# Turning the attention's value product round: probabilities stationary, values moving, the division after the product

## The chip, the cores and the metric

The kernel runs on one core of a Trainium2 chip. The metric is the device time of one execution in microseconds (us), as a median over several executions. One core has TensorE (PE; its weight loads are listed apart as PEld), VectorE (DVE), ScalarE (ACT), GpSimd (POOL) and SyncE (SP), which here issues the DMAs. Each engine takes its instructions in program order and waits on semaphores.

## What is computed

Two groups of rows, 1024 prompt rows and 32 sample rows, run through one attention layer and one gated linear recurrence, with norms and output projections around them. All is fp32. The part that matters is the core of the attention, for 8 query heads of width 128 that share 2 key and value heads (4 query heads each):

```python
logits = jnp.einsum('btkgd,btskd->btkgs', qg, k_sel).astype(f32) * ATT_SCALE
logits = jnp.where(valid[:, :, None, None, :], logits, -jnp.inf)
probs = jax.nn.softmax(logits, axis=-1).astype(v.dtype)
o = jnp.einsum('btkgs,btskd->btkgd', probs, v_sel)
...
return (o.reshape(B, L, ATT_WIDTH) * jax.nn.silu(z)) @ w_out
```

Each row attends to the 256 (sample: 136) keys that an indexer picks. The kernel does this densely with a mask, over all keys up to the row's block.

## The kernel before, in words

The program is a row of stages, each a block that ends before the next begins: input norm, attention projections (with the index scores and the search of the thresholds), attention, attention output, recurrence, final output. The change is in `attention`.

The stage walks over 72 items: 9 row tiles t (8 of 128 prompt rows, t = 0 to 7, and the sample's 32 rows, called tile S below), and 8 heads in each. A prompt tile t sees t+1 blocks of 128 keys, the sample 4 cached blocks and one of 32 keys. Every engine runs one loop over steps i, written out by hand, and works in step i on items that lie further and further back:

- PE, step i: the logits of item i (`multiply`, L843; q stationary, keys move, into `wide`); the transposes of the probabilities of item i-4 (`transpose`, L856, one per key block, into banks 0 and 1); and a quarter of a value product (`mix`, L872). `mix` works on a group of 4 heads that share a value head: v's block of 128x128 is stationary, and the four heads' transposed probabilities, 4x128 columns, move. The product comes out transposed (value column by row), as the output projection needs it.
- DVE, step i: `shift(i)` (L929) adds the mask, writes the row of logits to the SBUF ring `probs` and takes its extreme; then one of eight operations of `marking`, which makes the next tile's mask (L905 to L919); then `divide(i-2)`: a reciprocal of one column (L937) and a product of the whole row of probabilities with it (L939); every fourth step `gate` (L945), which multiplies a group's output in PSUM with the gate path.
- ACT, step i: the exponential of item i with its sum (L969), then the copies of the transposed probabilities of item i-4 from PSUM to `pT` (L979).

`multiply(i)` waits for `shift(i-2)`, since there are two halves of `wide`; `transpose` waits for `divide`; `mix` waits for the copies of its group. SP loads each tile's q and, once, the output weights. POOL works in this stage on two pieces of weights only (L200).

Of the kernel before, what the change touches and what calls it, by code (L numbers as in the profile page):

```python
# [16 lines left out]
ALU = mybir.AluOpType  # L17
# [757 lines left out]
def attention(nc, S):  # L775
# [23 lines left out]
    inv_done, probs_ready, pT_ready, pT_out = sem("inv_done"), sem("probs_ready"), sem("pT_ready"), sem("pT_out")  # L799
# [8 lines left out]
    q = space("q_tile", [P, 2, HEADS, P])  # L808
    with nc.Block() as block:
# [20 lines left out]
        def _(pe):  # L830
# [16 lines left out]
            def transpose(i):  # L847
                t, h = items[i]
                r = rows(t)
                pe.wait_ge(probs_ready, i + 1)  # L850
# [9 lines left out]
            def mix(g, quarter):  # L860

                t, h = items[4 * g]
                kv, r = h // GROUP, rows(t)
                if quarter == 0:
                    pe.wait_ge(pT_out, first_bank[4 * g + 4])
                    if g >= 2:
                        pe.wait_ge(gated, g - 1)
                n = (keys(t) + P - 1) // P
                for j in range((n * quarter + 3) // 4, (n * (quarter + 1) + 3) // 4):
                    kr = key_rows(t, j)  # L870
                    src = cv[:, j] if t == SAMPLE and j < PAST // P else v[0:kr, SAMPLE if t == SAMPLE else j]
                    last = pe.matmul(ps[2 + g % 2][:, 0:4 * r].rearrange("p (g q) -> p g q", g=4),  # L872
                                     src[:, kv * HD:(kv + 1) * HD], pT[0:kr, g % 2, j, :, 0:r],
                                     start=j == 0, stop=j == n - 1)
                    if j == n - 1:
                        last.then_inc(mixed, 1)

            for i in range(N + LAG + 4):
                if i < N:
                    multiply(i)  # L880
                if 0 <= i - LAG < N:
                    transpose(i - LAG)
                if i >= LAG + 4:
                    mix((i - LAG - 4) // 4, (i - LAG) % 4)

        @block.vector
        def _(dve):
# [45 lines left out]
            def divide(i):  # L933
                t, h = items[i]
                r, n = rows(t), keys(t)
# [13 lines left out]
            for i in range(N + 12):  # L949
# [7 lines left out]
                if 2 <= i <= N + 1:  # L957
                    divide(i - 2)
# [864 lines left out]
```

## Time and profile before

| | |
|---|---|
| three executions | 1550.73, 1551.94, 1554.93 us; median 1551.94 |
| profiled execution, first to last instruction (span) | 1547.9 us |
| granted TensorE clock, mean over the span | 0.960 of full speed |
| busy, share of the span | PE 91%, PEld 79%, DVE 62%, ACT 36%, POOL 33% |
| attention, first logits to last gate | 496.7 to 689.7 us, 193.0 us |
| PE busy in it | 181.2 us |
| DVE busy in it | 154.5 us |

Of the profiled execution the page gives its span; what lies outside the first and last instruction is the 4.0 us between it and the median, and nothing else of it is shown. A row of the profile gives an engine, a line of the program, an operation, the tiles it writes and reads, a count and durations. PE's durations are modelled ends of pipelined instructions, so the pace of a run of them is read from the starts.

### The profile page before, as it was taken

The numbers are of one execution on the slowest core, as the hardware profiler recorded it, in microseconds if no ns is written. First come the engines' busy times: TensorE is split into PE (matmuls) and PEld (weight loads), VectorE is DVE, ScalarE is ACT, GpSimd is POOL, SyncE is SP. The second block draws the span as 40 slices with busy tenths as digits, with TensorE's granted clock in tenths as the row PEclk, the third lists the DMA queues.
The fourth block names the chain that finished last, engine by engine and source line by source line (L and its number), as shares of the span: only waits on it lengthen the run. The fifth ranks groups of instructions, "written<-read, shape, count | busy, mean of one in ns | idle before, by whom it ended". The sixth has DMA issues, their size and how long they took to land. (4 is left out here: it accounts for less than half of the span.)

```text
span 1547.9 us, 21333 instructions
## 1 busy us (share of the span) xinstructions
PE 1402.9 (91%) x8109; PEld 1224.0 (79%) x8109; DVE 965.9 (62%) x1864; ACT 560.5 (36%) x1004; POOL 508.8 (33%) x404
## 2 busy tenths in 40 slices
PE   4999999999993899999979999999999999925898
PEld 3999647999992455548869999999999999914686
DVE  7011488999998989744550466475665566596332
ACT  6233463333322555541121444342525253340111
POOL 4276402355541001100020364544536163363000
PEclk9999999999996999999999999999999999957899
DMA  6121100232211410002231111010211110500221
GB/s 217 28 55 41 28 1 15 78 95 85 65 53 42 149 28 14 4 28 82 82 89 43 56 29 47 28 61 20 61 41 42 36 40 20 193 4 1 82 99 62
DMA packets 96180, 86.78 MB, mean 56 GB/s; under 512 B 4528, under 2 KB 84272, under 8 KB 96080
## 3 DMA queue, kind: packets, MB, share of 16 engines
q1 hardware_dynamic: 94448, 80.60, 16.9%
q0 software_dynamic: 1632, 4.82, 0.9%
q8 instruction: 66, 1.08, 0.3%
q14 instruction: 34, 0.28, 0.1%
HBM read 65.43 MB, written 19.97 MB: 55 GB/s over the span
## 5 line engine op out<-in xcount | busy, mean ns | idle before, releaser
L186 PE MATMUL bank<-hn_hi,rw_hi 128*128 128x352 f32 x768 | 250.3, 326 | 2.9 <-PEq L1009 2.9
L186 PE MATMUL bank<-hn_hi,rw_lo 128*128 128x352 f32 x768 | 247.2, 322 | 0.0
L186 PE MATMUL bank<-hn_lo,rw_hi 128*128 128x352 f32 x768 | 246.9, 322 | 0.0
L186 PE MATMUL bank<-hn_hi,w_hi 128*128 128x352 f32 x672 | 218.9, 326 | 3.6 <-PEq L274 3.6
L186 PE MATMUL bank<-hn_lo,w_hi 128*128 128x352 f32 x672 | 216.5, 322 | 0.0
L186 PE MATMUL bank<-hn_hi,w_lo 128*128 128x352 f32 x672 | 216.4, 322 | 0.0
L714 DVE TENSOR_SCALAR_CACHE_REDUCE marks<-score,bits 128x384 bf16<-128x384 f32 (+6 forms) x217 | 185.1, 917 | 3.7
L186 PEld LDWEIGHTS bank<-hn_hi,rw_hi 128*128 128x128 f32 x768 | 144.6, 188 | 4.6 <-POOL rw_lo L1145 3.1
L186 PEld LDWEIGHTS bank<-hn_lo,rw_hi 128*128 128x128 f32 x768 | 145.0, 189 | 0.0
L186 PEld LDWEIGHTS bank<-hn_hi,rw_lo 128*128 128x128 f32 x768 | 144.6, 188 | 0.0
L186 PEld LDWEIGHTS bank<-hn_hi,w_hi 128*128 128x128 f32 x672 | 127.0, 189 | 4.3 <-issue 3.7
L186 PEld LDWEIGHTS bank<-hn_lo,w_hi 128*128 128x128 f32 x672 | 127.2, 189 | 0.0
L186 PEld LDWEIGHTS bank<-hn_hi,w_lo 128*128 128x128 f32 x672 | 126.8, 189 | 0.0
L641 POOL TENSOR_TENSOR swapped<-swapped,sin 128x352 f32<-128x352 f32 x57 | 54.0, 947 | 187.8 <-ACT swapped L589 122.1
L1573 DVE TENSOR_TENSOR levels<-levels,q_rec 128x528 f32<-128x528 f32 (+1 forms) x48 | 101.4, 2177 | 1.9 <-ACT levels L1409 1.9
L843 PE MATMUL wide<-kT,q_tile 128*128 128x512 f32 (+3 forms) x192 | 75.4, 506 | 27.1 <-DMA q_tile<-q_rotated 26.9
L239 POOL TENSOR_SCALAR stats<-stats 128x1 f32<-128x1 f32 (+1 forms) x27 | 7.4, 273 | 279.4 <-ACT junk L1116 162.6
L1328 PE MATMUL wide<-levels 128*128 128x128 f32 (+1 forms) x832 | 98.2, 274 | 0.6
L1328 PEld LDWEIGHTS wide<-levels 128*128 128x128 f32 (+1 forms) x832 | 92.7, 185 | 6.0 <-issue 0.9
L1145 POOL TENSOR_TENSOR rw_lo<-rw_raw,rw_hi 128x1024 fp32r<-128x1024 f32 x32 | 76.0, 2386 | 59.6 <-ACT rw_hi L1138 59.5
L215 POOL TENSOR_TENSOR w_lo<-w_raw,w_hi 128x1024 fp32r<-128x1024 f32 x30 | 71.7, 2390 | 50.4 <-ACT w_hi L208 50.3
L843 PEld LDWEIGHTS wide<-kT,q_tile 128*128 128x128 f32 x192 | 36.6, 202 | 65.1 <-issue 34.2
(221 smaller groups left out, 2823.2 us busy)
## 6 DMA issues: line engine op xcount, KB each, us to landing
rw_raw<-in_rec_w_in SPq DMA_DIRECT2D x32, 512.0 KB, 4.1
w_raw<-in_att_w_in SPq DMA_DIRECT2D x30, 512.0 KB, 3.9
q_rotated<-relu SPq DMA_DIRECT2D x24, 176.0 KB, 1.9
xin<-in_x_prompt SPq DMA_DIRECT2D x8, 512.0 KB, 4.2
q_tile<-q_rotated SPq DMA_DIRECT2D x8, 512.0 KB, 3.7
wo_raw<-in_att_w_out SPq DMA_DIRECT2D x4, 1024.0 KB, 9.1
x_again<-in_x_prompt SPq DMA_DIRECT2D x8, 512.0 KB, 4.0
residual<-h_rows SPq DMA_DIRECT2D x8, 512.0 KB, 2.9
```

Source lines behind the costliest of these rows:

```text
L186: last = pe.matmul(out, l, r, start=n == 0, stop=n == len(passes) - 1)
L215: pool.tensor_tensor(S["w_lo"][:, slot], S["w_raw"][:, slot], S["w_hi"][:, slot].bitcast(F32), ALU.subtract).then_inc(S["w_lo_done"], 1)
L239: pool.tensor_scalar(stats[0:r, 1, t:t + 1], stats[0:r, 0, t:t + 1], 1.0 / D, EPS, ALU.mult, ALU.add).then_inc(pool_order, 1)
L641: pool.tensor_tensor(swapped[:, r % 3, :], swapped[:, r % 3, :], sin[:, part * CW:(part + 1) * CW], ALU.mult).then_inc(sin_done, 1)
L714: step(dve.tensor_scalar(marks[0:r, i % 2, 0:keys(t)], tile(i, t), bound, 0.0, op, ALU.add, accum_out=counts[0:r, first + i:first + i + 1]))
L843: last = pe.matmul(logits[0:rows(t), i % 2, a:e], q[:, t % 2, h, 0:rows(t)], src[:, h // GROUP, a:e], start=True, stop=True)
L1145: pool.tensor_tensor(S["rw_lo"][:, slot], S["rw_raw"][:, slot], S["rw_hi"][:, slot].bitcast(F32), ALU.subtract).then_inc(S["rec_lo_done"], 1)
L1328: last = pe.matmul(out[:, 0:r], left, right, start=True, stop=True)
L1573: dve.tensor_tensor(x, x, level_view(q[:, slot], m)[:, :, 1, :], ALU.mult).then_inc(q_scaled, 1)
```

## The change

The value product is done per head and not per group. For each head and key block the transposed probabilities (keys by 128 rows) are stationary and the 128 value columns move, so that the output stands row by value column in a quarter of the group's bank. The probabilities are no longer divided: `divide` now takes four reciprocals at once for a group, and a new DVE operation `scale` multiplies the group's output by them on its way from PSUM to `o_rows`. PE then turns the four 128x128 blocks back with four transposes (`turn`) into the same bank, from which `gate` reads as before. `transpose` waits for the exponential itself. The lags change too: `mix(i-6)` for one item in each step, `turn` in every fourth step, `divide`, `scale` and `gate` at other places of DVE's loop, and PE has one step more.

```diff
@@ PE @@
             def transpose(i):
-                pe.wait_ge(probs_ready, i + 1)
+                pe.wait_ge(exp_done, i + 1)
...
-            def mix(g, quarter):
-                if quarter == 0:
-                    pe.wait_ge(pT_out, first_bank[4 * g + 4])
-                    if g >= 2:
-                        pe.wait_ge(gated, g - 1)
-                for j in range((n * quarter + 3) // 4, (n * (quarter + 1) + 3) // 4):
-                    last = pe.matmul(ps[2 + g % 2][:, 0:4 * r].rearrange("p (g q) -> p g q", g=4),
-                                     src[:, kv * HD:(kv + 1) * HD], pT[0:kr, g % 2, j, :, 0:r],
-                                     start=j == 0, stop=j == n - 1)
+            def mix(i):
+                g, kv, r = i // GROUP, h // GROUP, rows(t)
+                pe.wait_ge(pT_out, first_bank[i + 1])
+                if g >= 2 and h % GROUP == 0:
+                    pe.wait_ge(gated, g - 1)
+                for j in range(n):
+                    last = pe.matmul(ps[2 + g % 2][0:r, (h % GROUP) * HD:(h % GROUP + 1) * HD],
+                                     pT[0:kr, g % 2, j, h % GROUP, 0:r], src[:, kv * HD:(kv + 1) * HD],
+                                     start=j == 0, stop=j == n - 1)
+                if h % GROUP == GROUP - 1:
+                    last.then_inc(mixed, 1)
+
+            def turn(g):
+                pe.wait_ge(scaled, g + 1)
+                for x in range(GROUP):
+                    last = pe.transpose(ps[2 + g % 2][:, x * r:(x + 1) * r], o_rows[0:r, g % 2, x, :], ident[0:r, 0:r])
+                last.then_inc(turned, 1)
 
-            for i in range(N + LAG + 4):
+            for i in range(N + LAG + 5):
...
-                if i >= LAG + 4:
-                    mix((i - LAG - 4) // 4, (i - LAG) % 4)
+                if 0 <= i - LAG - 2 < N:
+                    mix(i - LAG - 2)
+                if i >= LAG + 7 and (i - LAG - 7) % GROUP == 0:
+                    turn((i - LAG - 7) // GROUP)
@@ DVE @@
-            def divide(i):
-                dve.wait_ge(exp_done, i + 1)
-                dve.reciprocal(low[0:r, 2, i:i + 1], low[0:r, 1, i:i + 1]).then_inc(inv_done, 1)
-                dve.wait_ge(inv_done, i + 1)
-                dve.tensor_scalar(probs[0:r, i % RING, 0:n], probs[0:r, i % RING, 0:n], low[0:r, 2, i:i + 1], None,
-                                  ALU.mult).then_inc(probs_ready, 1)
+            def divide(g):
+                dve.wait_ge(exp_done, GROUP * (g + 1))
+                dve.reciprocal(low[0:r, 2, of], low[0:r, 1, of]).then_inc(inv_done, 1)
+
+            def scale(g):
+                dve.wait_ge(inv_done, g + 1)
+                dve.wait_ge(mixed, g + 1)
+                dve.tensor_tensor(o_rows[0:r, g % 2], ps[2 + g % 2][0:r, :].rearrange("p (g d) -> p g d", g=GROUP),
+                                  low[0:r, 2, of].unsqueeze(2).to_broadcast([r, GROUP, HD]), ALU.mult).then_inc(scaled, 1)
 
             def gate(g):
-                dve.wait_ge(mixed, g + 1)
+                dve.wait_ge(turned, g + 1)
...
-                if 2 <= i <= N + 1:
-                    divide(i - 2)
-                if i >= 12 and i % 4 == 0:
-                    gate((i - 12) // 4)
+                if i >= 6 and i % 4 == 2 and i - 6 < N:
+                    divide((i - 6) // 4)
+                if i >= 10 and i % 4 == 2:
+                    scale((i - 10) // 4)
+                if i >= 13 and i % 4 == 1:
+                    gate((i - 13) // 4)
```

How the order moves on PE, in two steps of tile 6 (out<-moving,stationary, and the columns that move; before, L843 are logits, L856 transposes, L872 the value product):

```order
L843 MATMUL wide<-kT,q_tile 128x512
L843 MATMUL wide<-kT,q_tile 128x384
L856 MATMUL bank<-ident,probs 128x128 x7
L872 MATMUL bank<-pT,v 128x512
L843 MATMUL wide<-kT,q_tile 128x512
L843 MATMUL wide<-kT,q_tile 128x384
L856 MATMUL bank<-ident,probs 128x128 x7
L872 MATMUL bank<-pT,v 128x512 x2
```

And now, with the lines shifted (L845 logits, L858 transposes, L873 value product, L884 the turn):

```order
L845 MATMUL wide<-kT,q_tile 128x512
L845 MATMUL wide<-kT,q_tile 128x384
L858 MATMUL bank<-ident,probs 128x128 x6
L873 MATMUL bank<-v,pT 128x128 x6
L884 MATMUL bank<-ident,o_rows 128x128 x4
L845 MATMUL wide<-kT,q_tile 128x512
L845 MATMUL wide<-kT,q_tile 128x384
L858 MATMUL bank<-ident,probs 128x128 x7
L873 MATMUL bank<-v,pT 128x128 x6
```

One or two products of 512 columns in a step have become one product of 128 columns for each key block, and once in four steps four transposes follow.

DVE in the steps of tile 3, before (ISA rows are `shift` and its accumulator; L937 and L939 the division, L945 the gate, L915 to L917 marking):

```order
L929 ISA probs,low<-wide,score 128x512
L929 ISA low 128x1
L915 TENSOR_TENSOR select_state<-limits,counts 128x1
L937 RECIPROCAL low<-low 128x1
L939 TENSOR_SCALAR probs<-probs,low 128x512
L929 ISA probs,low<-wide,score 128x512
L929 ISA low 128x1
L916 SCALAR_TENSOR_TENSOR ranks<-marks 128x640
L937 RECIPROCAL low<-low 128x1
L939 TENSOR_SCALAR probs<-probs,low 128x512
L945 TENSOR_TENSOR qiT_zT_gT<-bank,qiT_zT_gT 128x4x128
```

And in the changed kernel at the end of tile 3 (L940 `shift`, L929 and L930 marking, L947 four reciprocals, L953 `scale`):

```order
L940 ISA probs,low<-wide,score 128x512
L940 ISA low 128x1
L929 SCALAR_TENSOR_TENSOR ranks<-ranks,marks 128x640
L947 RECIPROCAL low<-low 128x4
L953 TENSOR_TENSOR o_rows<-bank,low 128x512
L940 ISA probs,low<-wide,score 128x512
L940 ISA low 128x1
L930 TENSOR_SCALAR score<-ranks 128x640
```

The two rows of a division in every step are gone; one reciprocal and one scaling stand in one step of four.

## Rows read from the trace of the kernel before

**Rows 1.** The page: busy time of each engine, its share of the span, instructions.

```profile
PE 1402.9 (91%) x8109; PEld 1224.0 (79%) x8109; DVE 965.9 (62%) x1864; ACT 560.5 (36%) x1004; POOL 508.8 (33%) x404
```

**Rows 2.** Stretches (tiles 0-7, S, tail): length; busy PE, PEld, DVE, ACT, POOL; PEclk; DMA.

```profile
496.70:501.90 5.20, 5.20 (x20) 4.50 (x21) 3.58 (x24) 3.55 (x16) 0.00 (x0) 0.50 0.16 48
501.90:512.70 10.80, 8.84 (x35) 4.80 (x33) 9.80 (x41) 5.65 (x25) 0.00 (x0) 0.96 0.18 49
512.70:527.00 14.30, 12.24 (x46) 6.19 (x45) 13.64 (x46) 7.74 (x25) 0.00 (x0) 1.00 0.91 330
527.00:544.60 17.60, 15.87 (x57) 8.02 (x57) 16.89 (x47) 10.28 (x27) 0.00 (x0) 1.00 0.11 31
544.60:566.60 22.00, 20.11 (x87) 11.94 (x86) 20.54 (x49) 12.26 (x29) 0.00 (x0) 1.00 0.09 25
566.60:591.20 24.60, 24.27 (x98) 13.91 (x97) 21.79 (x46) 13.51 (x33) 0.00 (x0) 1.00 0.08 23
591.20:622.00 30.80, 28.46 (x109) 15.69 (x108) 26.93 (x46) 16.98 (x34) 4.54 (x1) 1.00 0.07 18
622.00:655.30 33.30, 32.59 (x121) 17.31 (x119) 26.06 (x45) 18.80 (x34) 4.52 (x1) 1.00 0.02 3
655.30:684.20 28.90, 28.51 (x117) 12.94 (x116) 13.49 (x38) 13.25 (x36) 0.00 (x0) 1.00 0.00 1
684.20:689.70 5.50, 5.11 (x41) 3.97 (x40) 1.79 (x5) 1.33 (x8) 0.00 (x0) 1.00 0.00 0
```

**Rows 3.** Waits, 492 to 690 us: who waited for whom, total us, times, longest.

```profile
DVE probs L929 <- PE wide L843: 33.7, 28, 5.4
PEld bank L856 <- DVE probs L939: 11.9, 17, 2.4
```

**Rows 4.** Timeline of PE, one step of tile 7: start, duration, instructions.

```profile
643.17 1.88 PE L843 MATMUL wide<-kT,q_tile 128*128 128x512 f32 x4
644.89 1.04 PE L856 MATMUL bank<-ident,probs 128*128 128x128 f32 x8
645.76 1.88 PE L872 MATMUL bank<-pT,v 128*128 128x512 f32 x4
647.48 1.88 PE L843 MATMUL wide<-kT,q_tile 128*128 128x512 f32 x4
```

**Rows 5.** A load's group (busy, mean ns), and runs of 128-column products with own loads.

```profile
L1328 PEld LDWEIGHTS wide<-levels 128*128 128x128 f32 (+1 forms) x832 | 92.7, 185 | 6.0 <-issue 0.9
...
914.34 11.80 PEld L1328 LDWEIGHTS wide<-levels 128*128 128x128 f32 x101
...
687.83 0.97 PEld L872 LDWEIGHTS bank<-pT,cache_v 128*128 128x128 f32 x8 [0.28 <-ACT pT L979]
687.83 1.16 PE L872 MATMUL bank<-pT,cache_v 128*128 128x128 f32 x8
```

**Rows 6.** Groups by line, 492 to 690 us: the division.

```profile
L939 DVE TENSOR_SCALAR probs<-probs,low 128x128 f32<-128x128 f32 (+8 forms) x72 | 43.2, 600 | 2.5
```

**Rows 7.** Timeline of DVE, end of a step of tile 2: division and gate.

```profile
523.43 0.16 DVE L937 RECIPROCAL low<-low 128x1 f32<-128x1 f32 x1
523.63 0.42 DVE L939 TENSOR_SCALAR probs<-probs,low 128x384 f32<-128x384 f32 x1
523.96 0.69 DVE L945 TENSOR_TENSOR qiT_zT_gT<-bank,qiT_zT_gT 128x512 f32<-128x512 f32 x1
524.56 0.55 DVE L929 CUSTOM_DVE_ANT_0 probs<-wide,score 128x384 f32<-128x384 f32 x1
```

**Rows 8.** Timeline: a division in tile 7 beside POOL's work, and PE's wait.

```profile
629.17 4.52 POOL L200 TENSOR_TENSOR wo_lo<-wo_raw,wo_hi 128x2048 fp32r<-128x2048 f32 x1 [26.86 <-ACT wo_hi L193]
...
630.29 3.89 DVE L939 TENSOR_SCALAR probs<-probs,low 128x896 f32<-128x896 f32 x1
...
637.18 0.75 PEld L856 LDWEIGHTS bank<-ident,probs 128*128 128x128 f32 x7 [1.51 <-DVE probs L939]
```

**Rows 9.** Timeline: the last gate of the stage.

```profile
689.44 0.29 DVE L945 TENSOR_TENSOR qiT_zT_gT<-bank,qiT_zT_gT 128x128 f32<-128x128 f32 x1 [1.37 <-PE bank L872]
```

More of the change, by code:

```diff
@@ L798, in attention @@
     logits_ready, logits_read, exp_done = sem("logits_ready"), sem("logits_read"), sem("exp_done")
-    inv_done, probs_ready, pT_ready, pT_out = sem("inv_done"), sem("probs_ready"), sem("pT_ready"), sem("pT_out")
+    inv_done, scaled, turned, pT_ready, pT_out = sem("inv_done"), sem("o_scaled"), sem("o_turned"), sem("pT_ready"), sem("pT_out")
     mixed, gated, order = sem("mixed"), sem("gated"), sem("mark_order")
@@ L808, in attention @@
     q = space("q_tile", [P, 2, HEADS, P])
+    o_rows = space("o_rows", [P, 2, GROUP, HD])
+    assert space.at <= S["third_at"]
     with nc.Block() as block:
@@ L858, in transpose @@
                     last.then_inc(pT_ready, 1)
-            def mix(g, quarter):
-                t, h = items[4 * g]
-                kv, r = h // GROUP, rows(t)
-                if quarter == 0:
-                    pe.wait_ge(pT_out, first_bank[4 * g + 4])
-                    if g >= 2:
-                        pe.wait_ge(gated, g - 1)
+            def mix(i):
+                t, h = items[i]
+                g, kv, r = i // GROUP, h // GROUP, rows(t)
+                pe.wait_ge(pT_out, first_bank[i + 1])
+                if g >= 2 and h % GROUP == 0:
+                    pe.wait_ge(gated, g - 1)
                 n = (keys(t) + P - 1) // P
-                for j in range((n * quarter + 3) // 4, (n * (quarter + 1) + 3) // 4):
+                for j in range(n):
                     kr = key_rows(t, j)
                     src = cv[:, j] if t == SAMPLE and j < PAST // P else v[0:kr, SAMPLE if t == SAMPLE else j]
-                    last = pe.matmul(ps[2 + g % 2][:, 0:4 * r].rearrange("p (g q) -> p g q", g=4),
-                                     src[:, kv * HD:(kv + 1) * HD], pT[0:kr, g % 2, j, :, 0:r],
+                    last = pe.matmul(ps[2 + g % 2][0:r, (h % GROUP) * HD:(h % GROUP + 1) * HD],
+                                     pT[0:kr, g % 2, j, h % GROUP, 0:r], src[:, kv * HD:(kv + 1) * HD],
                                      start=j == 0, stop=j == n - 1)
-                    if j == n - 1:
-                        last.then_inc(mixed, 1)
-            for i in range(N + LAG + 4):
+                if h % GROUP == GROUP - 1:
+                    last.then_inc(mixed, 1)
+            def turn(g):
+                r = rows(items[GROUP * g][0])
+                pe.wait_ge(scaled, g + 1)
[3 more added lines that the diff above has]
+            for i in range(N + LAG + 5):
                 if i < N:
@@ L947, in gate @@
                                   gT[:, h:h + 4, span(t)], ALU.mult).then_inc(gated, 1)
-            for i in range(N + 12):
+            for i in range(N + 10):
                 if i < N:
```

4 lines of the change are left out of this document (2 added, 2 removed).

## The prediction, made before the changed kernel ran

> **What bounds the kernel now.** First the page: PE is busy for 91% of the span, DVE for 62% [rows 1]. Such a share is a mean over stages, so the attention stage is cut at the first logits of each tile [rows 2]; the reader should compare PE and DVE in each stretch. In tiles 1 to 4 DVE is busy for 9.80 of 10.80, 13.64 of 14.30, 16.89 of 17.60 and 20.54 of 22.00 us, and PE less: DVE sets the pace there. From tile 5 on PE does (24.27 of 24.60, 32.59 of 33.30). In tile 0 PE is busy all the time at a granted clock of 0.50, the lower level of 1.2 GHz, so PE sets the pace there too. The waits agree: DVE waits 33.7 us for logits, and PE's loads wait 11.9 us, in 17 waits, for the divided probabilities [rows 3].
>
> PE's price for one step is read from starts [rows 4]. In tile 7 the logits take 644.89 - 643.17 = 1.72 us, the eight transposes 0.87 (0.11 each), the value product 1.72, together 4.31. The four instructions of 512 columns are two products of the program, since each fp32 product is two instructions (the order has L872 twice where the profile shows four). That is 0.427 us for each instruction and 0.853 for a key block and a group; 128 columns are a quarter of an instruction, 0.107.
>
> **The change on PE.** A key block and group now takes eight instructions of 128 columns, each with its own weights. The trace has such pairs. In the recurrence a load lasts 0.185 us, yet 101 of them take 11.80, each with its product; without the last one's duration that is 0.116 us each. At the end of the attention, in the sample's value product, 8 take 0.97 by the loads, 0.111 each, and by the products, where the last lasts 0.27, 1.16, or 0.126 [rows 5]. I take 0.115, next to the long run; bounds 0.111 and 0.126. A key block of one head is then 0.23 us, of a group 0.92 against 0.853. That is all the finer cut costs in prompt tiles: 72 key blocks and groups x 0.067 = 4.8 us.
>
> These rows also answer a rule that speaks against the change: the load goes on beside the product before it, as one pair each 0.116 us shows where the load alone lasts 0.185. The Trainium skill, TensorE: Matmul & The Clock Gate, in "Packing small matmuls", says that weight loads overlap running products only where their row groups differ, and these do not differ. By it load and product would stand one behind the other, and the sum would be some 65 us higher; the trace has it otherwise, and it is the second rival.
>
> The turn adds 16 x 4 transposes of 0.11, so 7.0 us in prompt groups.
>
> **By tile.** In prompt tile t, PE issued eight logits (0.213 a key block), 8t+4 transposes, and both groups of tile t-1: 1.707(t+1) + 0.11(8t+4) + 1.707t. Now it issues 0.23(8t+2) for the value product (six items of tile t-1, two of t) and two turns of 0.44. The sum goes from 2.15 + 4.29t to 3.49 + 4.43t us: from 6.4, 10.7, 15.0, 19.3, 23.6, 27.9, 32.2 in tiles 1 to 7 to 7.9, 12.3, 16.8, 21.2, 25.6, 30.0, 34.5.
>
> **The change on DVE.** 72 divisions go (43.2 us [rows 6]) and 72 reciprocals of 0.16, 11.5. 18 reciprocals and 18 scalings come; the nearest row to a scaling is the gate, of the same width and from PSUM too, 0.69 [rows 7]: 15.3 us at most. DVE is relieved of some 40 us. Where DVE sets the pace this counts; where PE does it counts only by PE's waits. By the starts, reciprocal and division of 384 columns take 523.96 - 523.43 = 0.53 us and a gate 0.60 [rows 7]; a key block more or less is 0.07. Tile 2 divides two items of 256 columns and six of 384, so it loses 2 x 0.46 + 6 x 0.53 = 4.1 us and gains twice 0.20 + 0.60: 2.5 net. Tiles 1 and 3 likewise have 2.0 and 3.1. DVE then needs 8.8, 11.8 and 14.5: PE's new work is as long or longer from tile 2 on, and PE becomes the bound nearly everywhere.
>
> New lengths, where I add 0.1 to 0.6 for steps in which marking is long and DVE is late: tile 1 9.6 (between DVE's 8.8 and the 7.9 of PE, whose first two steps still have the low clock), tile 2 12.9, 3 17.1, 4 21.4, 5 25.8, 6 30.2, 7 34.6. Before: 10.8, 14.3, 17.6, 22.0, 24.6, 30.8, 33.3 [rows 2]. That is -1.2, -1.4, -0.5, -0.6, +1.2, -0.6, +1.3, together -1.8.
>
> Tile 6 shortens because it carries a stall that goes. Its 30.8 us held only 28.46 of PE's work [rows 2], and its longest wait for a division was 2.4 us [rows 3]. In tile 7, beside POOL's work on the weights, a division lasted 3.89 us where the mean is 0.60, and PE's loads waited 1.51 [rows 6, 8]; the other such piece of POOL's lies in tile 6 [rows 2]. The Trainium skill, SBUF — State Buffer, "Who interferes with whom", says that VectorE and GpSimd share a pair of ports, which one instruction holds to its end; by it a tensor_scalar of marking could inherit the wait, and DVE now has more than 1 us of room in each step of these tiles, so the sum would stay.
>
> Tile 0: the first two items' value products now fall into it, 2 x 0.46 at 1.2 GHz, +0.9. S: PE had 8 half groups of tile 7, 13.65 us, and has six items of tile 7 (6 x 1.84), two of the sample (2 x 5 blocks x 0.23) and two turns (0.88), 14.2: +0.6. The waits in it I leave.
>
> The tail: there the cost is bare, since nothing is left to overlap. Sample blocks had moved 4x32 = 128 columns for four heads at once; now 128 value columns move for each head, four times the instructions (80 for 20). After the last logits stood 5.5 us. Now come four sets of transposes (4 x 0.39), six value products (6 x 1.15) and a turn (0.4), 8.9 us, and behind the last product, which ends some 0.2 after its start, scale (0.65 with its wait), turn (0.6 with its latency) and gate (0.29) in a chain, in place of the gate alone [rows 9]: 1.8. Scale's and turn's times are my estimates from the gate and the transposes with 0.2 of latency. Together 10.7, +5.2.
>
> **The sum.** +0.9 - 1.8 + 0.6 + 5.2 = +4.9 us on 193.0. Nothing else of the program changes; the output stage starts later by the same. The profiled span would go from 1547.9 to 1552.8, and with the 4.0 us between span and median unchanged the time is 1551.94 + 4.9 = 1556.8. Bounds: with 0.111 or 0.126 for the pair the sum is 2.6 lower or 7 higher over 656 instructions, of which tiles 0 and 1 hide some of the latter.
>
> **Rivals.** *The relief returns more than I count.* With 0.111 a pair (-2.6), and PE in tiles 2 to 7 without any lost time (-1.4), the sum is +0.9: 1552.8, within the 0.3%. For it: from tile 5 on nearly every wait of PE was on a division, and the exponential is done two steps before the transpose needs it. Against: tile 5, hardly stalled, already ran 1.0 us over the worked content. It decides if tile 7 takes under 34.4 us. Chance 0.40, counting the lower half of my own spread.
>
> *The load is not hidden.* If a changed stationary operand in each pair cost its load, 0.107 beside 0.107, the 656 instructions would take 65 us more, less what tiles 1 to 3 absorb: about 1615. Against it stand all of rows 5. Chance 0.03.
>
> *A new wait between PE and DVE.* The first product of a group now waits for a gate that DVE does one step before, where there were four steps between. In tiles 1 to 3 DVE's step with scan or gate (about 2 us) is as long as PE's step; if PE then waits 0.5 us in each of eight groups, the sum is +9: 1561. It shows as waits of L873 on L959. Against: DVE also has less to do in just these steps. Chance 0.10.
>
> *Faster.* If PE, denser in the tail, kept the high clock into the output stage, about 2 us would come back, and with the first rival a gain could show. Chance 0.06.
>
> **How the numbers follow.** A measurement of this kernel tells about 0.3%, 4.7 us, from no change. My sum lies on that edge, so "slower" (my case's upper half 0.38, the two slow rivals 0.13) has 0.51; "same" has 0.42; "faster" 0.07 with the scatter of the runs, which is 4 us wide. The range 1551 to 1563 takes in the first rival below, and the new wait and the 0.126 pair above; it leaves the unhidden load out.
>
> **What would show it.** Pairs of the value product at 0.115 us; a step of tile 7 at 4.42 + 0.11; tiles 1 and 2 shorter by over 1 us each and tiles 5 and 7 longer; DVE busy near 115 us in the stage and waiting for logits from tile 2 on; waits of transposes on DVE gone; a tail near 10.7. Wrong: pairs near 0.19, waits of L873 on the gate, or a tail under 9.

## The result, and the profile after

| | before | changed |
|---|---|---|
| executions | 1550.62 to 1554.93 us, median 1551.34 (4) | 1559.32 to 1559.50 us, median 1559.41 (4) |
| ratio to before | | 1.0050, 95% interval 1.0038 to 1.0062 |
| span of the profiled execution | 1547.9 us | 1557.5 us |
| attention, first logits to end of the last gate | 193.0 us | 199.9 us |

The change costs 8.1 us by the medians, 5.9 to 9.6 by the interval, so it is slower beyond the 0.3%. In the two profiled executions 6.9 us of the difference lie in the attention. Of the rest, 0.8 lie ahead of it and 2.0 behind it, where both kernels are the same. From the last gate to the end passed 858.1 us before and 860.1 after, and 858.0 to 860.6 in the experiments, which are also the same there: that part moves by as much from one execution to another.

The stretches of the changed kernel, cut at the first logits of each tile as in [rows 2] (length; then busy PE, PEld, DVE, ACT, POOL; granted clock; DMA):

```profile
497.50:503.10 5.60, 5.57 (x24) 4.90 (x25) 2.31 (x16) 3.77 (x17) 0.00 (x0) 0.55 0.21 63
503.10:514.30 11.20, 8.87 (x58) 6.94 (x57) 9.21 (x34) 6.39 (x25) 0.00 (x0) 1.00 0.17 48
514.30:528.60 14.30, 12.73 (x82) 9.81 (x81) 11.70 (x34) 8.31 (x26) 0.00 (x0) 1.00 0.92 332
528.60:546.30 17.70, 17.11 (x106) 12.47 (x105) 13.76 (x33) 9.91 (x27) 0.00 (x0) 1.00 0.13 33
546.30:567.70 21.40, 21.38 (x146) 17.27 (x145) 15.77 (x33) 11.70 (x29) 0.00 (x0) 1.00 0.10 28
567.70:593.20 25.50, 25.50 (x172) 20.69 (x170) 17.80 (x33) 13.83 (x33) 0.00 (x0) 1.00 0.10 27
593.20:622.90 29.70, 29.70 (x194) 23.33 (x193) 20.97 (x33) 17.09 (x34) 4.54 (x1) 1.00 0.06 15
622.90:657.10 34.20, 34.20 (x218) 26.05 (x216) 17.77 (x32) 19.03 (x35) 4.54 (x1) 1.00 0.00 0
657.10:686.20 29.10, 29.10 (x215) 21.66 (x213) 8.50 (x23) 11.94 (x34) 0.00 (x0) 1.00 0.00 1
686.20:697.50 11.30, 10.04 (x86) 7.23 (x85) 2.50 (x6) 1.33 (x8) 0.00 (x0) 1.00 0.01 1
```

From tile 4 to S PE is busy without a gap, which it was not before. In tiles 1 and 2 neither engine is: in tile 1 PE is busy for 8.87 of 11.20 and DVE for 9.21. Both wait, and that is the part that the forecast did not have:

| stretch | before | forecast | measured |
|---|---|---|---|
| tile 0 | 5.2 | 6.1 | 5.6 |
| tile 1 | 10.8 | 9.6 | 11.2 |
| tile 2 | 14.3 | 12.9 | 14.3 |
| tile 3 | 17.6 | 17.1 | 17.7 |
| tiles 4, 5, 6, 7 | 22.0, 24.6, 30.8, 33.3 | 21.4, 25.8, 30.2, 34.6 | 21.4, 25.5, 29.7, 34.2 |
| S | 28.9 | 29.5 | 29.1 |
| tail | 5.5 | 10.7 | 11.3 |
| sum | 193.0 | 197.9 | 200.0 |

(The cuts are rounded to 0.1 us, so the stretches add up to 200.0 and not 199.9.)

The waits of the changed kernel in this stage (total, times, longest), of which the first three had no counterpart before, and the transposes' wait, now on the exponential, answers to [rows 3]:

```profile
PE bank L873 <- DVE qiT_zT_gT L959: 3.4, 5, 1.3
PEld bank L884 <- DVE o_rows L953: 2.0, 2, 1.1
DVE o_rows L953 <- PE bank L873: 5.2, 2, 2.7
DVE probs L940 <- PE wide L845: 36.4, 26, 5.1
PEld bank L858 <- ACT probs L985: 1.5, 5, 0.6
```

The value product waits for gates 3.4 us in five waits, and the turn for the scaling. The transposes' 11.9 us of waits on the division have become 1.5.

A piece of tile 1 shows how the two engines wait for each other in turn. PE of the changed kernel:

```profile
505.76 0.70 PE L845 MATMUL wide<-kT,q_tile 128*128 128x256 f32 x2
507.90 0.66 PE L884 MATMUL bank<-ident,o_rows 128*128 128x128 f32 x4 [0.74 <-DVE o_rows L953]
508.39 0.60 PE L845 MATMUL wide<-kT,q_tile 128*128 128x256 f32 x2
...
510.59 0.41 PE L858 MATMUL bank<-ident,probs 128*128 128x128 f32 x2
512.29 0.68 PE L873 MATMUL bank<-v,pT 128*128 128x128 f32 x4 [1.29 <-DVE qiT_zT_gT L959]
```

And DVE in the same time:

```profile
507.17 0.68 DVE L953 TENSOR_TENSOR o_rows<-bank,low 128x512 f32<-128x512 f32 x1
507.76 0.42 DVE L940 CUSTOM_DVE_ANT_0 probs<-wide,open_mask 128x256 f32<-128x256 f32 x1
508.10 0.15 DVE L926 TENSOR_TENSOR select_state<-limits,counts 128x1 f32<-128x1 f32 x1
509.12 0.42 DVE L940 CUSTOM_DVE_ANT_0 probs<-wide,open_mask 128x256 f32<-128x256 f32 x1 [0.87 <-DVE select_state L926]
509.47 0.95 DVE L927 TENSOR_TENSOR_SCAN ranks<-marks 128x384 f32<-128x384 bf16 x1
510.81 0.61 DVE L928 SCALAR_TENSOR_TENSOR ranks<-ranks,select_state,marks 128x384 f32<-128x384 f32 x1
511.46 0.69 DVE L959 TENSOR_TENSOR qiT_zT_gT<-bank,qiT_zT_gT 128x512 f32<-128x512 f32 x1
```

The turn waits until the scaling of 507.17 ends, and the logits of the next item stand behind it in PE's order until 508.39. So DVE, whose shift at 509.12 needs those logits, stands for 0.87 us (the releaser given there is an instruction of DVE itself; the logits of 508.39, with 0.60 us, end just ahead of it). Then the scan, the next marking operation and the gate follow one another on DVE, and PE's value product waits 1.29 us for that gate.

The tail, first the last value products and then the chain behind them:

```profile
694.42 1.06 PE L873 MATMUL bank<-cache_v,pT 128*32 128x128 f32 x8
695.41 0.40 PE L873 MATMUL bank<-v,pT 32*32 32x128 f32 x2
696.65 0.43 PE L884 MATMUL bank<-ident,o_rows 32*128 32x32 f32 x4 [0.84 <-DVE o_rows L953]
```

```profile
695.92 0.68 DVE L953 TENSOR_TENSOR o_rows<-bank,low 32x512 f32<-32x512 f32 x1 [2.42 <-PE bank L873]
697.12 0.29 DVE L959 TENSOR_TENSOR qiT_zT_gT<-bank,qiT_zT_gT 128x128 f32<-128x128 f32 x1 [0.52 <-PE bank L884]
```

From the end of the last product, 695.81, to that of the gate, 697.41, pass 1.6 us, where before the gate of [rows 9] alone followed.

The pace of the pairs, in tile 7, from the starts of value product and next logits:

```profile
622.94 1.88 PE L845 MATMUL wide<-kT,q_tile 128*128 128x512 f32 x4
624.66 0.93 PE L858 MATMUL bank<-ident,probs 128*128 128x128 f32 x7
625.42 1.73 PE L873 MATMUL bank<-v,pT 128*128 128x128 f32 x14
```

The next logits start at 626.99, so 14 pairs take 1.57 us, 0.112 each. Here the kernel does not wait for its weight loads.

### The profile page after: what moved, and what is told of

It is laid out like the page before. It is cut to its first block and busy times, and to the rows that moved or that the text cites. A ratio compares the mean times of both kernels' runs of the same rounds, so it can differ in the third digit from the quotient of the medians.

```text
span 1557.5 us, 22342 instructions
## 1 busy us (share of the span) xinstructions
PE 1416.9 (91%) x8673; PEld 1276.3 (82%) x8673; DVE 932.1 (60%) x1756; ACT 560.7 (36%) x1004; POOL 507.9 (33%) x404
## 3 DMA queue, kind: packets, MB, share of 16 engines
q8 instruction: 71, 1.16, 0.3%
## 5 line engine op out<-in xcount | busy, mean ns | idle before, releaser
L186 PE MATMUL bank<-hn_hi,w_lo 128*128 128x352 f32 x672 | 216.3, 322 | 0.0
L845 PE MATMUL wide<-kT,q_tile 128*128 128x512 f32 (+3 forms) x192 | 74.4, 501 | 26.8 <-DMA q_tile<-q_rotated 26.7
L985 ACT ACTIVATE probs<-probs,low 128x128 f32<-128x128 f32 (+8 forms) x72 | 55.6, 773 | 88.5 <-DVE low L940 88.5
```

The lines of the kernel that those rows point to most:

```text
L186: last = pe.matmul(out, l, r, start=n == 0, stop=n == len(passes) - 1)
L845: last = pe.matmul(logits[0:rows(t), i % 2, a:e], q[:, t % 2, h, 0:rows(t)], src[:, h // GROUP, a:e], start=True, stop=True)
L985: act.activation(probs[0:r, i % RING, 0:n], probs[0:r, i % RING, 0:n], ACT.Exp, scale=-1.0, bias=low[0:r, 0, i:i + 1], accum_out=low[0:r, ...
```

## The experiments

Eleven kernels ran beside executions of the kernel before on the same chip (median 1551.3 to 1552.0). For comparison between them I cut each stage at the first shift of DVE in each tile, which is later than the first logits by 0.6 to 2.6 us (before and changed), and give four parts: tiles 0 to 3; 4 and 5; 6 and 7; and S with the tail. "Stage" goes from the first logits, which are 0.8 us ahead of the first shift. These parts come from one profiled execution of each kernel; the medians and ratios come from all of its executions.

| kernel | 0-3 | 4, 5 | 6, 7 | S and tail | stage | median | ratio, 95% interval |
|---|---|---|---|---|---|---|---|
| before | 49.2 | 21.3, 24.8 | 31.0, 32.6 | 33.2 | 193.0 | 1551.34 | |
| changed | 49.4 | 21.6, 25.6 | 30.0, 33.4 | 39.0 | 199.9 | 1559.41 | 1.0050 (1.0038-1.0062) |
| gate_early | 47.8 | 22.1, 26.0 | 30.0, 33.5 | 39.0 | 199.2 | 1557.68 | 1.0038 (1.0024-1.0051) |
| turn_late | 47.3 | 21.6, 25.6 | 30.0, 33.5 | 39.7 | 198.5 | 1556.54 | 1.0039 (1.0025-1.0053) |
| turn_twice | 52.3 | 22.5, 26.5 | 30.9, 34.3 | 40.4 | 207.7 | 1567.07 | 1.0098 (1.0084-1.0112) |
| no_division | 43.9 | 21.1, 24.6 | 28.5, 31.7 | 33.2 | 183.9 | 1542.57 | 0.9941 (0.9928-0.9955) |
| product_only | 42.4 | 20.6, 24.8 | 29.1, 32.6 | 36.6 | 186.9 | 1543.49 | 0.9947 (0.9933-0.9961) |
| layout_alone | 55.7 | 23.1, 26.7 | 35.1, 35.9 | 39.0 | 216.3 | 1575.64 | 1.0151 (1.0138-1.0165) |
| sample_old | 47.2 | 22.1, 26.0 | 30.0, 33.4 | 33.2 | 192.8 | 1551.55 | 1.0003 (0.9994-1.0012) |
| both_mends | 47.3 | 21.6, 25.6 | 30.0, 33.5 | 36.2 | 195.0 | 1553.21 | 1.0006 (0.9997-1.0015) |
| pool_division | 44.7 | 20.8, 24.4 | 33.5, 32.6 | 34.1 | 190.9 | 1550.34 | 0.9993 (0.9984-1.0002) |
| pool_moved | 45.2 | 20.8, 24.4 | 28.4, 32.3 | 36.8 | 188.7 | 1545.16 | 0.9962 (0.9950-0.9975) |
| pool_in_tile7 | 44.7 | 20.8, 24.4 | 28.4, 32.6 | 35.8 | 187.5 | 1546.57 | 0.9969 (0.9957-0.9981) |

Two things are to be kept in mind when single tiles are compared. First, tile 0 starts at a granted clock of 0.50 in every run, and the clock rises to 1.00 at some point between 500.1 and 504.5 us. The changed kernel, gate_early, turn_late and turn_twice do the same work in tile 0, yet it lasted 5.4, 5.7, 5.1 and 5.7 us. So up to 0.6 us in "0-3" is the moment of that rise. Second, before and changed then stay at 1.00 to the last gate, but in some experiments the clock fell back to 0.50, each time in a wait of PE or soon behind one: in layout_alone at 508.5 and 614.3 us (tiles 1 and 6), in pool_division at 609.0 (tile 6), in pool_moved at 651.2 (S), in both_mends at 681.1 and in sample_old at 685.6 (tail), and in the last microsecond of the three kernels with POOL. In pool_moved:

```profile
650.23 1.07 PE L861 MATMUL bank<-ident,probs 128*128 128x128 f32 x8 [2.04 <-POOL probs L831]
651.14 3.51 PE L877 MATMUL bank<-pT,v 128*128 128x512 f32 x4
```

The product behind the wait takes 3.51 us, where [rows 4] has 1.88 for the same four instructions. A wait of 2.04 us so cost 1.6 us more than its length.

### Is PE the bound: turn_twice

```diff
-                for x in range(GROUP):
+                for x in 2 * list(range(GROUP)):
                     last = pe.transpose(ps[2 + g % 2][:, x * r:(x + 1) * r], o_rows[0:r, g % 2, x, :], ident[0:r, 0:r])
```

> The changed kernel with every turn done twice (the four transposes of a group are repeated into the same places). Theory A: PE has no idle time from tile 2 on, so each of some 14 groups costs its 0.44 us and the stage grows by 6 to 7.5 us over 200.0. Theory B: PE's busy share is an artefact of modelled ends and DVE or ACT set the pace in the middle tiles; then the stage grows by under 4.

Measured: stage 207.7, +7.8. Tiles 4 to 7 grew by 0.9 each, which is two turns of 0.44, and S with the tail by 1.4. Even tiles 0 to 3 grew by 2.9, for the six turns in them. Theory A holds, a little above its range: from tile 4 on PE is the bound, and a turn costs at least its own time everywhere. In tiles 1 to 3, where PE has gaps, this shows only that the turn lies on the path, not that PE is full.

### The distances: gate_early and turn_late

gate_early:

```diff
-                if i >= 13 and i % 4 == 1:
-                    gate((i - 13) // 4)
+                if i >= 12 and i % 4 == 0:
+                    gate((i - 12) // 4)
```

> The changed kernel with the gate of a group one DVE step earlier (step 4g+12 in place of 4g+13), nothing else. Theory A: the 3.4 us that PE's value product waited for gates (5 waits in tiles 1 to 3) are the loss there, because PE needs the gate one step after DVE does it; with one step more of distance these waits go and the attention stage shortens from 200.0 us by 2.5 to 3.5, all in tiles 1 to 3 (11.2 + 14.3 + 17.7 to about 40), the time to about 1556.5. Theory B: DVE's uneven steps are the loss and the gate is only where it shows; the wait moves to another place and the stage stays within 0.8 us.

turn_late:

```diff
-            for i in range(N + LAG + 5):
+            for i in range(N + LAG + 6):
...
-                if i >= LAG + 7 and (i - LAG - 7) % GROUP == 0:
-                    turn((i - LAG - 7) // GROUP)
+                if i >= LAG + 8 and (i - LAG - 8) % GROUP == 0:
+                    turn((i - LAG - 8) // GROUP)
```

> The changed kernel with each turn one PE step later, at the end of step 4g+12 in place of 4g+11; the gate stays. In the changed kernel the turn waited for the scaling twice in tiles 0 to 2 (2.0 us by the loads) and held back the logits behind it, so that DVE stood too; the value product waited 3.4 us for gates. Theory A: both waits are one coupling, PE and DVE are late for each other in turn; taking the turn's away shortens tiles 1 to 3 (43.2 us) by 1 us and leaves the gate's, total about -1. Theory B: only the gate's distance matters: within 0.5 us of the changed kernel. Against both: the later turn makes the gate later, its wait grows and the stage gets longer by over 1 us.

With the early gate the value product's waits on gates are gone from the long waits. Those of the turn on the scaling grew:

```profile
PEld bank L884 <- DVE o_rows L953: 3.8, 5, 1.1
PE bank L884 <- DVE o_rows L953: 2.8, 5, 0.8
```

Tiles 0 to 3 lost 1.6 us (tiles 1 to 3 alone 1.8), tiles 4 and 5 took 0.9 of them back: stage -0.7. My theory A asked for 2.5 to 3.5 and fell; B, that the wait moves, is nearer. With the late turn the same tiles lost 2.1 us (tiles 1 to 3 alone 1.8, of which 0.4 is one turn that now stands behind the cut, in tile 4), though most of the gate's wait stayed:

```profile
PE bank L873 <- DVE qiT_zT_gT L959: 2.6, 4, 1.1
PEld bank L884 <- DVE o_rows L953: 1.1, 1, 1.1
```

There theory A holds: -1.4 in the stage, or -1.1 without tile 0. Behind the sample's first shift 0.7 more stand, of which 0.4 is again a turn that the cut now leaves there. The ratios of the two kernels and of the changed one overlap (1.0024 to 1.0062), so these gains rest on the profiled executions alone. They say that the loss is no single wait. Between the last product of a group (step 4g+9) and the first product of the group that uses its bank next (step 4g+14) lie four steps, and PE hands over to DVE for the scaling, DVE to PE for the turn, PE to DVE for the gate, and DVE to PE for that product. More distance at one hand-over takes it from another.

### What each part costs alone: no_division, product_only, layout_alone

no_division (on the kernel before; it leaves out the division):

```diff
-                pe.wait_ge(probs_ready, i + 1)
+                pe.wait_ge(exp_done, i + 1)
...
-                if 2 <= i <= N + 1:
-                    divide(i - 2)
```

> The kernel before, with its order and its product, but the probabilities are never divided by their sums: the reciprocals and the 72 products are left out, and the transposes wait for the exponential. It measures the relief of DVE alone. Theory A: tiles 1 to 4 fall to about PE's content (8.8, 11.0, 15.2, 19.4), tile 6 loses its stall, and the stage goes from 193.0 to about 178.5 us, the time to about 1537. Theory B: what DVE does is mostly hidden and the relief is worth under 6 us, so that the new layout costs little.

Measured: stage 183.9, -9.1: 5.3 in tiles 0 to 3, 3.4 in tiles 6 and 7, where a division no longer stands beside POOL's weights, and nothing at the end. Neither theory's number holds (-14.5, under 6). PE's content, at which I took tiles 1 to 4 to run, was too low a floor: cut at the shifts they take 9.2, 12.7, 16.7 and 21.1 us, against 8.8, 11.0, 15.2 and 19.4. By tile the relief is 2.7, 2.1, 0.5 and 0.2, so DVE's division held up tiles 1 and 2, and hardly tiles 3 and 4, though DVE had been busy there for more of the time than PE. In tile 4 of no_division, PE still waits:

```profile
556.83 0.53 PEld L856 LDWEIGHTS bank<-ident,probs 128*128 128x128 f32 x5 [0.62 <-ACT probs L958]
556.86 0.74 PE L856 MATMUL bank<-ident,probs 128*128 128x128 f32 x5 [0.46 <-ACT pT L968]
```

The releasers point at a chain of shift, exponential, copy and transposes, with DVE's marking ahead of it, that is about as long as a step. That this chain sets the pace is my reading; no run shortens it.

product_only (on the changed kernel; it leaves out the division and the transposes back, and the gate waits for the product itself):

```diff
-                if i >= LAG + 7 and (i - LAG - 7) % GROUP == 0:
-                    turn((i - LAG - 7) // GROUP)
...
-                if i >= 6 and i % 4 == 2 and i - 6 < N:
-                    divide((i - 6) // 4)
-                if i >= 10 and i % 4 == 2:
-                    scale((i - 10) // 4)
-                if i >= 13 and i % 4 == 1:
-                    gate((i - 13) // 4)
+                if i >= 10 and i % 4 == 2:
+                    gate((i - 10) // 4)
```

> The changed kernel without reciprocals, scaling and turn: only the product in its new form, per head with 128 value columns moving; the gate reads its output where it stands. Left out are the division and the transposes back. To be set beside the kernel before without the division, 183.9 us, which differs by the product's form alone. Theory A: 72 key blocks and groups at the pace of the pairs, 0.224 us a head (14 pairs in 1.57 us in tile 7), against 0.853 give 3.1 us, and the sample's 60 further instructions 4 to 6: stage 191 to 193, of which 5 behind the first logits of S. Theory B: the pairs cost more where they alternate with the other work, or the load shows: stage over 196.

Measured: stage 186.9. That is 3.0 over no_division, less than either theory had: +3.4 behind the sample's first shift, +1.5 in tiles 6 and 7, and tiles 0 to 3 even 1.5 shorter. The likely cause is the place of the product: in no_division its loads waited 4.4 us, in eight waits, for the last copy of a group, made one step before, and in product_only, where every copy is two steps old, none of these waits is left. The product's new form is cheap; the ratios, 0.9941 and 0.9947, do not even tell the two kernels apart. From product_only to the changed kernel, which adds reciprocals, scaling and turn, the stage grows by 13.0:

| | 0-3 | 4 | 5 | 6 | 7 | S and tail |
|---|---|---|---|---|---|---|
| added | 7.0 | 1.0 | 0.9 | 0.9 | 0.9 | 2.4 |

In tiles 4 to 7 a turn costs 0.4 to 0.5 us, its own length. In tiles 0 to 3 the six turns of tiles 1 to 3 cost 7.0, 1.2 each: 2.6 are their length, and 4.4 the waits. In tile 0 itself the changed kernel is 0.8 shorter, as the clock rose earlier in it, so in tiles 1 to 3 the waits come to 5.1. No run parts the turn from the scaling.

layout_alone (the changed kernel; the division where it was):

```diff
-                pe.wait_ge(exp_done, i + 1)
+                pe.wait_ge(probs_ready, i + 1)
...
-                dve.tensor_tensor(o_rows[0:r, g % 2], ps[2 + g % 2][0:r, :].rearrange("p (g d) -> p g d", g=GROUP),
-                                  low[0:r, 2, of].unsqueeze(2).to_broadcast([r, GROUP, HD]), ALU.mult).then_inc(scaled, 1)
+                dve.tensor_copy(o_rows[0:r, g % 2],
+                                ps[2 + g % 2][0:r, :].rearrange("p (g d) -> p g d", g=GROUP)).then_inc(scaled, 1)
...
-                if i >= 6 and i % 4 == 2 and i - 6 < N:
-                    divide((i - 6) // 4)
+                if 2 <= i <= N + 1:
+                    divide(i - 2)
```

> The changed kernel with the division as before (each item's probabilities, before the transposes) and a plain copy in place of the scaling: the new layout and its turn without the relief of DVE. Theory A: DVE is the bound in tiles 1 to 4 with two copies of 0.6 us in each beside what it did before, PE from tile 5 on; stage about 208 us, 8 over the changed kernel and 15 over the one before. Theory B: the new lags tie PE and DVE so closely that DVE's and PE's times add in part; stage over 213 us.

Measured: stage 216.3, +23.3 over the kernel before, so theory B. Some 3.2 us of it are the lower clock behind two waits of PE, in tiles 1 and 6 (estimated from the same instructions at 1.00 in the same trace); without them the stage would stand at theory B's bound, 213. DVE is not full either: it is busy for 12.4 of 14.3, 15.5 of 16.6 and 17.9 of 19.7 us in tiles 1 to 3, so the two engines' times add in part. Its wait on the gate:

```profile
PE bank L873 <- DVE qiT_zT_gT L962: 12.7, 8, 3.0
```

and two of its divisions beside POOL's weights, in tiles 6 and 7, which grew by 5.1 and 2.5 over the changed kernel:

```profile
609.98 3.80 DVE L950 TENSOR_SCALAR probs<-probs,low 128x768 f32<-128x768 f32 x1
645.23 4.05 DVE L950 TENSOR_SCALAR probs<-probs,low 128x896 f32<-128x896 f32 x1
```

Behind the first of them PE waited 2.96 us for the gate, and the clock fell:

```profile
614.52 2.90 PE L873 MATMUL bank<-v,pT 128*128 128x128 f32 x12 [2.96 <-DVE qiT_zT_gT L962]
```

With the old lags a late gate had four steps to be late in; with the new ones it has one. Taking the division off is worth 9.1 us in the old order and 16.4 in the new one, some 13 of them without the lower clock. Together: relief -9.1, product +3.0, turn with scaling +13.0, sum +6.9. The three add up by construction, since each kernel is set against the one before it; in another order of the steps their sizes would differ, as the 16.4 shows.

### The tail: sample_old and both_mends

sample_old is gate_early with the sample's items done as before. The core of the edit:

```diff
-                if 0 <= i - LAG - 2 < N:
+                if 0 <= i - LAG - 2 < OLD:
                     mix(i - LAG - 2)
...
+                if i - LAG - 4 >= OLD:
+                    mix_group((i - LAG - 4) // 4, (i - LAG) % 4)
...
+                if OLD <= i - 2 < N:
+                    divide_item(i - 2)
```

OLD is 64, the sample's first item; mix_group is the old `mix`, divide_item the old `divide`, and for these items transposes and gates wait as they did.

> The kernel with the early gate (expected against that one, 1557.7 us), and the sample's eight items done as before the change: divided one by one, four heads' probabilities moving past the values, no scaling and no turn. Prompt items keep the new layout. Theory A: the tail's four times as many instructions and its chain of scale, turn and gate cost 5.8 us by the stretches (11.3 against 5.5); they come back: from the sample's first logits to the last gate about 33.5 us in place of 39.0, the time about 1552. Theory B: part of that tail stands where the next stage would wait anyway; under 3 us come back.

Measured: S and tail 33.2 in place of 39.0, as before the change; the time falls by 6.1 us to 1551.55, which is the kernel before. So all of the tail's 5.8 us is bare, as theory A says. That the 33.2 is the very figure of before is chance. From the sample's first product to the last gate the same instructions take 5.1 us before and 6.6 here, since the clock fell to 0.50 at 685.6 us. The eight products of [rows 5], 1.16 us there, show it:

```profile
686.60 2.08 PE L893 MATMUL bank<-pT,cache_v 128*128 128x128 f32 x8
```

Ahead of that, S is 1.5 us shorter than before: the products of six items of tile 7 are left to do there, where before two whole groups were.

both_mends is sample_old with the gate of the changed kernel and turn_late's turn: two edits, not one.

> The changed kernel with the turn a step later (which gave 1.4 us of stage) and the sample's items done as before the change (which gave 5.8 against the early gate). Theory A: they add, since one acts in tiles 0 to 3 and the other behind the first logits of S: stage 198.5 - 5.8 = 192.7, time within 0.2% of before. Theory B: the later turn of the last prompt group now holds the sample's first gate; then it loses over 1 us of it, stage over 193.7.

Measured: stage 195.0, S and tail 36.2, 3.0 over sample_old. That is theory B's number, but not its mechanism: the sample's first gate, at 688.01 us, waits for its own product, not for the turn. Before the sample's first product PE stood for 1.40 us, as the last prompt turn had moved out of that gap, and the clock fell 4.5 us earlier than in sample_old:

```profile
681.53 0.66 PE L861 MATMUL bank<-ident,probs 32*128 32x32 f32 x5 [1.40 <-ACT pT L1033]
682.12 1.11 PE L904 MATMUL bank<-ident,o_rows 128*128 128x128 f32 x4
```

The turn takes 1.11 us where it takes 0.66 at 1.00. From the sample's first product to the last gate the instructions of sample_old need 8.0 us here against 6.6, which is 1.4 of the 3.0; a turn that the cut leaves in S is another 0.4. The ratio 1.0006 and that of sample_old 1.0003 do not differ.

### A better place for the division: pool_division, pool_moved, pool_in_tile7

On the kernel before, `divide` on DVE keeps the reciprocal, and POOL multiplies:

```diff
+            for i in range(N):
+                if i in (6 * HEADS + 1, 7 * HEADS + 1):
+                    out_weights_lo(pool, S, i // HEADS - 6)
+                r, n = rows(items[i][0]), keys(items[i][0])
+                pool.wait_ge(inv_done, i + 1)
+                pool.tensor_scalar(probs[0:r, i % RING, 0:n], probs[0:r, i % RING, 0:n], low[0:r, 2, i:i + 1], None,
+                                   ALU.mult).then_inc(probs_ready, 1)
```

> The kernel before, with its layout and order, but the division of the probabilities is done by POOL, which stands idle in this stage; DVE keeps the reciprocal. It asks whether DVE's relief (9.1 us without any division) is to be had without the new layout. Theory A: POOL needs some 2.4 us for 1024 columns, by its own row for 128x1024, and has 4.2 us a step there, so it keeps up, and the stage goes to about 186 us, the time to about 1545. Theory B: DVE's marking operations wait whole POOL instructions, as one division did for 3.89 us beside POOL's weights, so DVE loses more than it gains: stage over 193 us, time over 1552.

Measured: stage 190.9, the time the same as before. Tiles 0 to 5 are 5.4 us shorter, as theory A has it, but tile 6 is 2.5 longer, with PE behind POOL there, and 1.4 us more of lower clock behind that wait:

```profile
599.63 4.54 POOL L200 TENSOR_TENSOR wo_lo<-wo_raw,wo_hi 128x2048 fp32r<-128x2048 f32 x1
604.14 10.06 POOL L831 TENSOR_SCALAR probs<-probs,low 128x896 f32<-128x896 f32 x3
608.69 1.14 PEld L861 LDWEIGHTS bank<-ident,probs 128*128 128x128 f32 x7 [3.75 <-POOL probs L831]
```

So the weights' pieces were moved, to items 60 and 67 (pool_moved) or 57 and 62 (pool_in_tile7):

```diff
-                if i in (6 * HEADS + 1, 7 * HEADS + 1):
-                    out_weights_lo(pool, S, i // HEADS - 6)
+                if i in (60, 67):
+                    out_weights_lo(pool, S, (60, 67).index(i))
```

> The kernel with the division on POOL, but POOL's two pieces of output weights (4.5 us each) stand before the divisions of items 60 and 67 in place of 49 and 57. In that kernel tile 6 took 33.5 us against 31.0 before, since POOL's divisions of 896 columns (2.84 us each, 3.9 us a step) had no room for a piece. Theory A: in the second half of tile 7 and in S POOL has room, tile 6 falls to about 29.5 us, the stage from 190.9 to about 187, the time to about 1546.5. Theory B: the divisions themselves hold DVE's marking up in tile 6, and moving the pieces moves the stall: under 1.5 us.

> As pool_moved, but POOL's two pieces of output weights stand before the divisions of items 57 and 62, so both in tile 7. In pool_moved the second piece, before item 67, cost 2.7 us behind the sample's first logits (36.8 us against 34.1). Theory A: in tile 7 POOL has 1.4 us of room in each step of 4.3, so a piece is made up in three steps and items lead their transposes by two; tile 7 stays at 32.5 and the part behind it goes back to 34: stage 186, time about 1543. Theory B: two pieces in one tile are too much, tile 7 grows by over 1.5 us and nothing is gained.

Measured: tile 6 at 28.4 in both. pool_moved 1545.16 us, ratio 0.9962; pool_in_tile7 1546.57, ratio 0.9969. Their intervals overlap, so which is better stays open. Both are longer behind S's first shift (36.8 and 35.8 against 34.1). In pool_in_tile7 the second piece is the cause: it runs from 651.2 to 655.7 us, and PE waits 1.35 for POOL at 658.6; there theory A, 34, failed. For pool_moved my expectation above named the wrong piece. PE's wait of 2.04 us at 650.23 stands behind the first piece, which ran from 641.9 to 646.4, and the lower clock behind it cost 1.6 more; behind the second piece PE waits for POOL no longer than in the other two kernels, 0.74. Both kernels beat the one before, by 6.8 and 5.4 us of the medians beside them, and the changed one by 13 to 14: the relief of DVE was worth having, and there was a cheaper way to it.

## Why the prediction was right, and where it was not

The forecast was 1556.8 and slower by 4.9 us; measured were 1559.41 and +8.1, inside the range. That the number came so near is in part luck: in the stage tiles 1 to 3 were 3.6 us over the forecast, the tail 0.6, and tiles 4 to 7, S and tile 0 were 1.2, 0.4 and 0.5 under it. Step by step:

- *What bounds the kernel*: right for the changed kernel from tile 4 on, where PE is busy throughout and turn_twice shows a price of 0.44 a turn. For the kernel before, "DVE sets the pace" in tiles 1 to 4 was read from the larger busy share; no_division shows it for tiles 1 and 2 only.
- *The pair's price*: 0.112 in tile 7, between the bound 0.111 and the 0.115 I took. The bound of 0.126 came from the first start of its run; the others there are 0.11 apart. The unhidden load did not come. The rule of the Trainium skill, TensorE: Matmul & The Clock Gate, in "Packing small matmuls", that loads overlap only across row groups, does not hold for these pairs: at 0.112 us each they run at the pace of a quarter of 512 columns, 0.107, and a twentieth more.
- *Tiles 4 to 7*: forecast 112.0, measured 110.8. Tile 7 came to 34.2, under the first rival's mark of 34.4: that rival had the pair's price right, 0.111 for 0.112, but not its sum, +0.9.
- *The step that failed*: "tile 1 9.6, tile 2 12.9, 3 17.1". Measured 11.2, 14.3 and 17.7, 3.6 more. I had taken the longer of the two engines' contents and added 0.1 to 0.6 for bursts, as if the other's work lay wholly beside it. In its place stood the third rival, a new wait between PE and DVE, which I gave 0.10 and a price of 4 us, by the gate alone. Its sign, waits of L873 on L959, is the one that the prediction listed under "Wrong", and it came: 3.4 us in five waits. But gate_early and turn_late show that the gate is one of several hand-overs, and product_only against the changed kernel prices all of them at 4.4 to 5.1 us beyond the turns' length. The mechanism was there and its size near; its chance was too low.
- *Tile 6's stall*: gone, as forecast (30.2, measured 29.7). With what the Trainium skill, SBUF — State Buffer, says in "Who interferes with whom" of the pair of ports, the trace agrees: beside POOL's first piece, 599.87 to 604.41 us, a marking operation inherited the wait, with room to hide it:

```profile
602.90 2.07 DVE L925 TENSOR_SCALAR marks<-score,select_state 128x1024 bf16<-128x1024 f32 x1
```

Before, the same instruction took 0.74.
- *The tail*: forecast +5.2, measured +5.8 (11.3), and sample_old returns all of it. The ten pairs of a sample item take 1.32 us (686.28 to 687.60), 0.132 each on the mean, not 0.115. The pair is not dearer there: the first eight start 0.109 apart, after 0.133 for the first. What I left out are two pauses, 0.20 us from the eighth start to the ninth, where the operands go from 128 rows to 32, and 0.20 from the tenth to the transposes. The chain behind took 1.6, forecast 1.8.
- *Tile 0*: +0.4 in place of +0.9, which is no test, as the same work lasted 5.1 to 5.7 us with the moment at which the granted clock rose (0.55 on the mean of this stretch against 0.50 before).
- Of the 8.1 us 6.9 are shown in the stage; the other 1.2 cannot be told from the scatter of the unchanged part, 858.1 to 860.6.

## What to carry to other kernels

Before an engine that sets the pace only in some stretches is relieved by giving work to another, set both contents side by side for each stretch: here the relief returned 9.1 us, and a turn and a scaling that go through both engines in turn cost 13.0. A larger busy share is not yet the bound: DVE's relief shortened tiles 3 and 4 by 0.5 and 0.2 us only. In a loop written out by hand, count the steps between a hand-over and the next use of its buffer: the hand-overs squeezed into four steps cost 4 to 5 us where both engines were nearly full, and nothing where one had room. A layout that moves fewer columns per weight load cost little in itself, but at the end of a stage, with 32 rows, it was paid in full. Here an idle engine, POOL, gave a relief that added nothing to the bound, once its own work stood elsewhere. And read the granted clock before a stretch is explained: two kernels that differ only in the steps of a turn and a gate ran the same last instructions in 6.6 and 8.0 us.

## What the runs showed of the hardware that was not expected

- Fp32 pairs of a 128x128 load and 128 moving columns start 0.112 us apart. With a stationary operand of 32 columns it is 0.109, though that load alone lasts 0.11 against 0.19: the smaller load hardly helps. Where the operands changed from 128 rows to 32, 0.20 us lay between two starts.
- GpSimd kept up with the product of probabilities and reciprocals. It took 2.85 us for 128x1024 fp32, and 2.52 for 128x896 in pool_moved, against VectorE's 0.75 for 1024:

```profile
L831 POOL TENSOR_SCALAR probs<-probs,low 128x1024 f32<-128x1024 f32 x8 | 22.7, 2846 | 4.4 <-DVE low L941 4.4
```

- Beside these products some of VectorE's marking slowed, a tensor_scalar of 1024 columns from 0.74 to 1.30 us, and in pool_moved its tile still became shorter, 28.4 us against 31.0. Beside POOL's piece of weights in pool_division both sides slowed, VectorE's scan from 2.29 to 3.78 us and the POOL product behind the piece from 2.52 to 4.50; that is the tile that grew:

```profile
L921 DVE TENSOR_TENSOR_SCAN ranks<-marks 128x1024 f32<-128x1024 bf16 x1 | 3.8, 3782 | 0.0
```

- The granted clock fell from 1.00 to 0.50 behind some waits of PE and made them dearer: by 1.6 us behind one of 2.04 in pool_moved, by 1.6 behind one of 2.96 in layout_alone. Behind one of 1.35 in pool_in_tile7 it stayed at 1.00.
